# Exponentials one step later, and the maximum ahead of an older scaling, in the attention loops of a decoder kernel

## The reference

```python
def windowed_gqa(q, k, v, sink):
    ...
    s = jnp.einsum('bnqhgd,bnjhd->bnhgqj', qb, kb).astype(F32) * (A_HEAD_DIM ** -0.5)
    ...
    s = jnp.where(valid[None, :, None, None], s, -jnp.inf)
    sk = sink.astype(F32).reshape(1, 1, A_KV_HEADS_2, A_GROUP, 1, 1)
    m = jnp.maximum(jnp.max(s, axis=-1, keepdims=True), sk)
    p = jnp.exp(s - m)
    p = p / (jnp.sum(p, axis=-1, keepdims=True) + jnp.exp(sk - m))
    out = jnp.einsum('bnhgqj,bnjhd->bnqhgd', p.astype(v.dtype), vb)
```

## Time and profile before

| | us |
|---|---|
| median of 3 runs | 2438.64 |
| profiled execution | 2439.75 |
| its span, first to last instruction | 2437.6 |
| TensorE busy | 2334.7 (96%) |
| vector engine busy | 1306.6 (54%) |
| ScalarE busy | 959.7 (39%) |
| GpSimd busy | 405.3 (17%) |

### The profile page before, as it was taken

One profiled execution on the slowest core, in us unless ns is written; L12 is line 12 of the kernel. 1 busy time (PEld: TensorE's weight loads), 2 busy tenths in 40 slices (PEclk: granted clock), 3 DMA queues, 4 the chain that ended last, 5 costly groups with the idle time before them and its releaser, 6 DMA issues.

```text
span 2437.6 us, 30359 instructions
## 1 busy us (share of the span) xinstructions
PE 2334.7 (96%) x11616; PEld 1842.7 (76%) x11616; DVE 1306.6 (54%) x1690; ACT 959.7 (39%) x1401; POOL 405.3 (17%) x431
## 2 busy tenths in 40 slices
PE   9998999999998979999998989999999999999998
PEld 7774667888886647888887757888887757788887
DVE  6447646665545575665456765433346674433333
ACT  4327853433323363443233353322223862333222
POOL 0003423110003123111003024101112002211010
PEclk9999999999999999999999999999999999999999
DMA  5211002222222112222223112222223202222222
GB/s 183 104 70 36 1 12 88 91 103 86 104 86 97 50 36 74 98 103 86 104 86 129 70 36 86 101 89 103 89 101 107 92 1 86 87 104 86 92 102 82
DMA packets 31493, 203.79 MB, mean 84 GB/s; under 512 B 4260, under 2 KB 5288, under 8 KB 7720
## 3 DMA queue, kind: packets, MB, share of 16 engines
q1 hardware_dynamic: 30104, 199.37, 23.0%
q10 hardware_dynamic: 1296, 3.15, 0.3%
HBM read 200.41 MB, written 2.10 MB: 83 GB/s over the span
## 4 chain that ended last, share of the span: by engine, by line
PE 81%; DVE 9%; ACT 6%; issue 3%; DMA 0%; ACTq 0%; SPq 0%; POOLq 0%; DVEq 0%
PE D L582 71%; PE D L698 2%; PE D L706 2%; DVE prob L1960 2%; DVE w_lo L1647 2%; ACT prob L1311 2%; PE X L684 2%; DVE xg L1681 2%; ACT w_hi L1108 1%; DVE h L1706 1%; ACT prob_t L1108 1%; PE X L690 1%; PE X L806 1%; ACT mid L1108 1%; ACT xg L1108 1%
## 5 line engine op out<-in xcount | busy, mean ns | idle before, releaser
L582 PE MATMUL D<-xg,w_hi 128*128 128x512 f32 x3184 | 993.8, 393 | 23.0 <-DVE xg L1681 16.6
L582 PE MATMUL D<-mid,w_hi 128*128 128x512 f32 x2308 | 714.3, 391 | 20.3 <-DVE w_lo L1647 9.3
L582 PEld LDWEIGHTS D<-xg,w_hi 128*128 128x128 f32 x3184 | 600.2, 189 | 155.7 <-DVE xg L1681 17.7
L1647 DVE TENSOR_TENSOR w_lo<-w_raw,w_hi 128x2048 fp32r<-128x2048 f32 (+2 forms) x210 | 459.6, 2190 | 360.5 <-ACT w_hi L1108 360.3
L582 PE MATMUL D<-xg,w_lo 128*128 128x512 f32 x1592 | 623.1, 391 | 0.0
L1108 ACT ACTIVATE w_hi<-w_raw 128x2048 fp32r<-128x2048 f32 (+2 forms) x210 | 355.5, 1693 | 485.0 <-PE D L582 480.6
L582 PEld LDWEIGHTS D<-mid,w_hi 128*128 128x128 f32 x2308 | 433.0, 188 | 115.9 <-issue 17.8
L582 PE MATMUL D<-mid,w_lo 128*128 128x512 f32 x1154 | 449.8, 390 | 0.0
L582 PEld LDWEIGHTS D<-xg,w_lo 128*128 128x128 f32 x1592 | 301.0, 189 | 63.3
L582 PEld LDWEIGHTS D<-mid,w_lo 128*128 128x128 f32 x1154 | 216.9, 188 | 45.3
L1706 DVE TENSOR_TENSOR h<-D,h 128x1024 f32 (+1 forms) x71 | 86.8, 1222 | 259.6 <-PE D L582 259.5
(11 more groups left out here) (282 smaller groups left out, 1821.8 us busy)
## 6 DMA issues: line engine op xcount, KB each, us to landing
w_raw<-in_weights SPq DMA_DIRECT2D x184, 1024.0 KB, 4.8
h<-in_x SPq DMA_DIRECT2D x4, 512.0 KB, 7.6
out_y<-h SPq DMA_DIRECT2D x4, 512.0 KB, 2.9
w_raw<-in_weights SPq DMA_DIRECT2D x2, 512.0 KB, 7.3
inv_cnt<-in_inv_cnt ACTq DMA_DIRECT2D x1, 1024.0 KB, 5.5
cos<-in_cos ACTq DMA_DIRECT2D x3, 256.0 KB, 4.4
sin<-in_sin ACTq DMA_DIRECT2D x3, 256.0 KB, 5.6
vec<-in_vec SPq DMA_DIRECT2D x1, 272.0 KB, 2.7
```

The source lines that it names most:

```text
L582: last = nc.tensor.matmul(out, w[a], x[b], start=start and k == 0, stop=stop and k == 2)
L1647: return nc.vector.tensor_tensor(out, x, f(high), ALU.subtract)
```

## The change

A table `EXP_LAG` sets by how many steps ScalarE's exponentials fall behind: 1 for nsa, swa and even, 0 for odd. ScalarE then takes the exponentials of unit s - 1 in step s, behind the copy of unit s - 3. The vector engine takes the maximum of unit s and then scales unit s - 2 (in odd still s - 1); the scaling is now the function `scale_unit`. GpSimd waits for `normed`, the end of the vector engine's scaling, where it waited for `inverted`, the reciprocal; in nsa it still multiplies by the gate on `inverted`. TensorE waits for the banks of D before the first compressed turn of the loop. `LAG` stays.

```diff
--- before.py
+++ after.py
@@ -85,6 +85,7 @@
 
 TILES = {"nsa": 8, "swa": 8, "even": 4, "odd": 4}
 BRANCHES = {"nsa": 2, "swa": 1, "even": 1, "odd": 1}
+EXP_LAG = {"nsa": 1, "swa": 1, "even": 1, "odd": 0}
 LAG = {"nsa": 3, "swa": 3, "even": 3, "odd": 2}
 SINK0 = {"swa": 0, "even": NSA_HEADS}
 
@@ -769,6 +770,9 @@
                         g = s // 3 + 1
                         if g == 3:
                             pe.wait_ge(c_evac, 3)
+                        else:
+                            for v in range(u, u + 2):
+                                pe.wait_ge(d_free[v % 2], v // 2 + 1)
                         compressed_turn(g, D[:, 3, :])
                     if 0 <= s - lag < count:
                         n = s - lag
@@ -1296,13 +1300,14 @@
                         if s >= lag + 2:
                             act.wait_ge(pv_done, a - 1)
                         copy(prob_t[:, a % 2, :, 0:w], D[:, 0:2, 0:w]).then_inc(evac, 1)
-                    if s < count:
-                        a = a0 + s
+                    if 0 <= s - EXP_LAG[kind] < count:
+                        n = s - EXP_LAG[kind]
+                        a = a0 + n
                         c, p = pair_of(a), probs(kind, a)
-                        w = len(key_blocks(kind, units[s][1])) * P + (kind in SINK0)
+                        w = len(key_blocks(kind, units[n][1])) * P + (kind in SINK0)
                         act.wait_ge(maxed, a + 1)
                         if kind in SINK0:
-                            act.wait_ge(sink_in, sinks_before[l] + s + 1)
+                            act.wait_ge(sink_in, sinks_before[l] + n + 1)
                         if kind == "odd" and s >= 2:
 
                             act.wait_ge(turned, a - 1)
@@ -1931,6 +1936,23 @@
                     gated_low(2)
                     gated_low(3)
 
+            def scale_unit(kind, l, units, n):
+
+                a = units_before[l] + n
+                t, qt, branch = units[n]
+                c, w = pair_of(a), len(key_blocks(kind, qt)) * P
+                dve.wait_ge(exped, a + 1)
+                nc.vector.reciprocal(inv_sum[:, c:c + 2], row_sum[:, c:c + 2]).then_inc(inverted, 1)
+                dve.wait_ge(inverted, a + 1)
+                for o in range(2 if kind == "odd" else 1):
+                    p = probs(kind, a)[:, o, 0:w]
+                    inv = inv_sum[:, c + o:c + o + 1]
+                    if kind == "nsa":
+                        ins = nc.vector.tensor_scalar(p, p, inv, gate_of(t, o, qt, branch), ALU.mult, ALU.mult)
+                    else:
+                        ins = nc.vector.tensor_scalar(p, p, inv, None, ALU.mult)
+                ins.then_inc(normed, 1)
+
             def attend(kind, l, u_out, n_late=None, u_late=None):
                 units, a0 = attention_units(kind), units_before[l]
                 count, per = len(units), QT * BRANCHES[kind]
@@ -1962,21 +1984,9 @@
                                     X[:, b + o, 0:w].rearrange(blocks, k=P), edge_masks(kind, units[s][1]),
                                     -1.0, least, ALU.add, ALU.min, neg_max[:, c + o:c + o + 1])
                         ins.then_inc(maxed, 1)
-                    if 0 <= s - 1 < count:
-                        a = a0 + s - 1
-                        t, qt, branch = units[s - 1]
-                        c, w = pair_of(a), len(key_blocks(kind, qt)) * P
-                        dve.wait_ge(exped, a + 1)
-                        nc.vector.reciprocal(inv_sum[:, c:c + 2], row_sum[:, c:c + 2]).then_inc(inverted, 1)
-                        dve.wait_ge(inverted, a + 1)
-                        for o in range(2 if kind == "odd" else 1):
-                            p = probs(kind, a)[:, o, 0:w]
-                            inv = inv_sum[:, c + o:c + o + 1]
-                            if kind == "nsa":
-                                ins = nc.vector.tensor_scalar(p, p, inv, gate_of(t, o, qt, branch), ALU.mult, ALU.mult)
-                            else:
-                                ins = nc.vector.tensor_scalar(p, p, inv, None, ALU.mult)
-                        ins.then_inc(normed, 1)
+                    n = s - 1 - EXP_LAG[kind]
+                    if 0 <= n < count:
+                        scale_unit(kind, l, units, n)
                     if s >= lag + 2 and (s - lag - 2) % per == per - 1:
 
                         t = (s - lag - 2) // per
@@ -2410,9 +2420,10 @@
                         a, (t, qt, branch) = a0 + s - 1, units[s - 1]
                         c, w = pair_of(a) + 1, len(key_blocks(kind, qt)) * P
                         p, inv = prob_4[:, a % 4, 1, 0:w], inv_sum[:, c:c + 1]
-                        pool.wait_ge(inverted, a + 1)
                         if kind == "nsa":
+                            pool.wait_ge(inverted, a + 1)
                             link(nc.gpsimd.tensor_tensor(inv, inv, gate_of(t, 1, qt, branch), ALU.mult))
+                        pool.wait_ge(normed, a + 1)
                         ins = nc.gpsimd.tensor_tensor(p, p, inv.to_broadcast([P, w]), ALU.mult)
                         ins.then_inc(second_normed, 1)
```

## The result

The kernel after took 2483.70 us (median of 4 runs, 2480.51 to 2488.95), the kernel before 2438.52 us beside it (4 runs, 2437.25 to 2445.00): 1.0181 times as long, 95% interval 1.0169 to 1.0193. That is 45.2 us slower; the forecast was 2475 us, 36.5 slower, in a range of 2452 to 2500. The profiled execution of after took 2480.51 us (span 2478.4), so the two traces are 40.8 us apart in span.

The account below looks back on a forecast made before the run. TensorE, 96% busy, was taken to bound the kernel. Longer chains were to add 18.5 us in nsa, 12 in swa and 6 in even, 36.5 on a median of 2438.64: 2475 us, range 2452 to 2500.

Parts of the forecast that it names:

- T waits for G, G for R, R for M of two units later: Changed stages: transposes wait for second-head scaling (GpSimd), that for reciprocal and first-head scaling, that for a later maximum; +36.5 us.
- Rival 1: swa and even: ending the mutual wait of vector engine and GpSimd makes the kernel faster, 2423 us; chance 0.09.
- the four legs: Successive stretches of an nsa tile between transposes of units numbered modulo 8; sum 20.8 us for 18.32, 19.8 over 8 tiles.
- The ends of the stage: nsa's start: TensorE should reach unit 0's transposes about 1.3 us earlier, leaving net +18.5 us.
- T7 to T1: nsa, transposes of unit 7 to those of the next unit 1: TensorE's own work, 4.92 us.
- T1 to T3: nsa, transposes of unit 1 to 3: copy, exponentials, mid copy and low part, maximum, tail; 5.33 us (swa 5.51).
- T3 to T5: nsa, transposes of unit 3 to 5: scores and maximum of unit 7, then tail; 5.34 us (swa 4.05).
- T5 to T7: nsa, transposes of unit 5 to 7: copy, exponentials until the reciprocal, tail; 5.21 us.
- Plain tiles: swa tiles without weight-split pieces: 9.56 us for 7.57, +2.0 each; three such tiles, +6.
- Rival 3: New stalls lower TensorE's clock; transposes, value products and scores double, +25 us over swa and even, 2500 us; chance 0.08.
- The weight pieces: Three swa tiles with next weight split: low piece collides with GpSimd's scaling, 1.05 us for 0.68; +1.3 each, 3.9.
- The tail: Reciprocal's start to transposes: 2.07, 1.74 or 1.41 us in nsa, 1.34 in swa; includes 0.08 from vector engine to GpSimd.

Follow-up runs that it names:

- g_behind_only: Kernel before, changed only so that GpSimd begins the second head's scaling after the vector engine's scaling ends: 2433.37 us, 0.9967 of before.
- lag4: Kernel after with only LAG changed, 3 to 4 in nsa, swa and even, so transposes come one step later: 2428.26 us, 0.9950 of before.
- lag4_mid_first: lag4 with ScalarE's mid copy also moved ahead of the exponentials of its step: 2427.58 us, 0.9954 of before.
- fill_stalls: Kernel after with unused matmuls added on TensorE in swa's two long stalls: 2483.81 us, 1.0189 of before.
- mid_first: Kernel after with ScalarE's mid copy moved ahead of the exponentials of its step, in all four stages: 2461.60 us, 1.0095 of before.
- lag4_alone: lag4 with the exponentials put back in their own step (EXP_LAG 0 everywhere): 2456.71 us, 1.0058 of before.

## Why the prediction was right, step by step

**Sign and mechanism.** Right. T waits for G, G for R, R for M of two units later; four experiments that each give the chain one piece of room (scaling first, mid copy first, GpSimd earlier, one step more) each take away a part of the loss, and the last all of it. Rival 1 (faster, 2423 us) is out; the gain that it counted on is there, 7 us of it, where the chain keeps its steps (g_behind_only).

**nsa, the four legs.** T7 to T1 4.90 us (forecast 4.92), T1 to T3 5.37 (5.33), T3 to T5 5.30 (5.34), T5 to T7 5.16 (5.21). Over 8 tiles 2.41 x 8 = 19.3 (19.8). The ends of the stage gave back 2.6 us and not 1.3: 19.3 less 16.7. "TensorE should get T(0) about 1.3 us earlier" was right: T(0) comes 5.17 us after the first scores (189.52), before 6.72 (191.39), so 1.55 earlier. What was mis-sized is the factor 8: from T(0) to T(7) after takes 21.13 us for 19.47, 1.7 more and not 2.4, the second tile costs 2.0, and the last one, which drains the pipeline, 3.3. lag4 and lag4_mid_first show how large the start is where the chain has room: from the first scores to the first mid copy they take 29.0 and 27.8 us, after 33.0 and before 33.5, with tiles no shorter than before.

**swa.** Forecast +12, measured +15.6. Plain tiles cost +2.6 (10.16 us for 7.57) instead of +2.0. The legs show where: T1 to T3 5.58 (5.51; T1 at 912.55, T3 at 918.13), T3 to T5 4.58 (4.05). The timeline of after, TensorE, behind T3:

```profile
907.97 0.63 PE L699 MATMUL D<-ident,prob 128*128 128x128 f32 x4 [1.68 <-DVE prob L1953]
...
909.11 1.10 PE L685 MATMUL X<-kd,q_all 64*128 64x256 f32 x4
910.15 0.69 PE L699 MATMUL D<-ident,prob 128*128 128x128 f32 x2
...
912.55 0.70 PE L699 MATMUL D<-ident,prob 128*128 128x128 f32 x4
```

The engine had stood for 1.68 us and waited 2.06 us for its weight load; the scores at 909.11 then take 1.10 us, where the same four take 0.70 at 905.58, and the two transposes 0.69 for 0.44. Rival 3, to which I gave 0.08, thus held for this stage, at a third of its price: 0.6 us a plain tile, not 1.9. Of the tiles with pieces that at 882.52 stayed at 1.00 and the ones on both sides of it (871.44, 893.44) had 0.85; nsa's middle tile stayed at 1.00. In fill_stalls all six tiles behind the first mid copy ran at 1.00 and cost 10.2 us more than before, for 9.9 forecast (6 and 3.9); in after they cost 13.8. The 3.7 us between the two are about the whole miss in swa. The Trainium skill, "TensorE: Matmul & The Clock Gate", Part 1, has the clock fall when the engine idles; the granted clock of 0.83 behind stalls of about 2 us agrees with it, and so does the 1.00 of fill_stalls, where the stalls are filled, while mid_first's plain tile, 8.60 us long with TensorE busy for 6.67, kept 1.00.

**The weight pieces.** This step failed. I wrote that the low piece would collide with G and take about 1.1 us. The groups of after from 850 to 942 us:

```profile
L2427 POOL TENSOR_TENSOR prob<-prob,inv_sum 128x256 f32<-128x256 f32 x24 | 18.0, 751 | 49.8 <-DVE prob L1953 49.8
...
L1953 DVE TENSOR_SCALAR prob<-prob,inv_sum 128x256 f32<-128x256 f32 x24 | 8.5, 353 | 0.9
...
L1652 DVE TENSOR_TENSOR w_lo<-w_raw,w_hi 128x512 fp32r<-128x512 f32 x8 | 5.5, 684 | 0.0
```

The piece takes 0.68 us as before, not 1.05 as in nsa, and the scaling 0.35 for 0.81; it is GpSimd's product that grew, from 0.61 to 0.75 us on average. The vector engine's piece starts at the scaling's end (885.61), GpSimd's product 0.17 us later, and of the two the later pays: 0.99 us, on the path to T, in four products of 256 keys (two of 128 keys take 0.78 for 0.40). In nsa before it was the other way round: the products began 0.08 to 0.15 us ahead of the piece (221.46 and 221.54) and kept their 0.85 and 1.13 us, and the piece took 1.31 to 1.53 us; 1.05 is the mean of four such pieces and four of 0.68 to 0.69. Two more of the 24 products took 1.52 us (857.79 and 860.05), each begun 0.17 us behind a rotary product of the vector engine of 1.22 us, a collision that the forecast did not have; what they cost on the path is not shown. The three tiles with pieces cost +2.4, +1.0 and +1.8 us, 5.2 in all, where 3.9 was forecast. In fill_stalls, at the full clock, they cost +1.3, +1.0 and +1.2, 3.4 in all: near in size, by another road, and the other 1.7 us go with the 0.85.

```profile
885.61 0.69 DVE L1652 TENSOR_TENSOR w_lo<-w_raw,w_hi 128x512 fp32r<-128x512 f32 x1
...
885.78 0.99 POOL L2427 TENSOR_TENSOR prob<-prob,inv_sum 128x256 f32<-128x256 f32 x1 [4.14 <-DVE prob L1953]
```

(The first row is of the vector engine's timeline in after, the second of GpSimd's.)

**even.** +5.5 for a forecast of 6, and that close in part by luck: the stage itself takes 7.2 us more and the layers behind it 1.7 less. A tile at the full clock (1451.74) takes 11.14 us for 10.02, forecast 10.8; the next takes 13.13 us for 9.90 at a granted clock of 0.74.

**Outside the stages.** Forecast 0, measured +3.3 from odd's mark to the end, 3.2 of it behind the stage; over the whole kernel the layers behind the stages sum to +0.3. In after the linear layers from 2067.5 to 2167.5 us ran at a granted clock of 0.97, the same stretch of before at 1.00. The four runs of after spread over 8 us, so some of this may be of the one execution only.

**The sum.** 18.5 + 12 + 6 = 36.5 was forecast; 16.7 + 15.6 + 5.5 + 3.3 - 0.3 = 40.8 measured in the traces, 45.2 between the medians. By stages the traces miss the forecast by -1.8, +3.6, -0.5, +3.3 and -0.3. The two that are too large are those with the lower clock: swa's tiles (3.7 us beside fill_stalls) and the layers behind odd. The median of after is 45.2 us above before's, where the traces are 40.8 apart: the profiled execution was the fastest of the four.

**The tail.** From the scaling's start (906.82) to GpSimd's (907.25) is 0.43 us: 0.35 and 0.08, as taken from before's gate product. That delay was the one number that the trace of before showed only for another pair, and it carried.

**What stays open.** Why the clock is lowered behind one stage and not behind another of nearly the same course was not settled; fill_stalls and lag4_mid_first show only that what a stage saves can come back behind it.

## What to carry to other kernels

A software pipeline has a distance in steps, and each stage put one step later needs its step of distance back: count the chain from the matmul that releases it to the matmul that takes it, queue by queue, before moving a stage. An engine that becomes freer (here the vector engine, 6.92 to 5.49 us a tile) says nothing of the end if its work now comes later. And a repair of contention that puts two operations one behind the other is to be given only where they do not lie on the path: alone it gained 0.3%, on the short chain it cost 0.4% in the traces and 0.9% between the medians (2483.70 for 2461.79 us), the clock's share included.

## What the runs showed of the hardware beyond this

- A scaling of 128x256 on the vector engine takes 0.81 us when GpSimd's product over 128x256 starts with it, 0.35 alone; GpSimd's product takes 0.61 alone and 0.99 when a product of two SBUF operands of the vector engine, 0.69 us long, has begun 0.17 us before it, 1.52 when one of 1.22 us has: both times it ends 0.47 us after the vector engine's. Where GpSimd began first, 0.08 us ahead (221.46, before), its product kept 0.85 us and the vector engine's took 1.32 for 0.68. The vector engine's maximum (0.48 us, scores from PSUM) beside it stretched neither.
- Of swa's plain tiles, all with the same work, those of 9.39, 9.67, 9.91 and 10.16 us had a granted clock of 0.80 to 0.83, and one of 9.57 us whose stalls were filled with idle matmuls 1.00. Those of 6.59 to 9.06 us had 1.00 but for one of lag4_alone, whose line is below; the length is in part the clock's own doing, and does not tell the clock.

```profile
897.46:905.91 8.45, 8.45 (x70) 5.31 (x68) 5.66 (x25) 6.59 (x22) 2.97 (x9) 0.88 0.00 1
```

- Ten microseconds of linear layers right behind swa ran at 0.83 in one kernel and at 1.00 in another, where the stage before had tiles of 6.59 and 6.95 us, both at 1.00 and with TensorE busy for 6.59 and 6.70.
